# A quarter of the tokens leaves the dense expert loop and gathers its expert rows instead

## The reference, cut to what matters

```python
def peer_ffn(h, ...):
    ...
    top_s, pos = lax.top_k(cand_s, PEER_TOPK)
    eid = jnp.take_along_axis(cand_i, pos, axis=-1)      # 128 expert numbers per token
    gate = jax.nn.softmax(top_s, axis=-1)
    ...
    a = jnp.einsum('td,tkd->tk', hb, peer_u[eb], preferred_element_type=jnp.float32)
    a = jax.nn.gelu(a, approximate=False)
    return jnp.einsum('tk,tkd->td', (gb * a).astype(hb.dtype), peer_v[eb])
```

## Time and profile before

| | us |
|---|---|
| median of 3 runs | 1116.73 (1114.97 to 1119.02) |
| the profiled execution | 1120.11, of which the span of the trace is 1118.3 |
| start up to the choice of experts | 0 to 200 |
| choice of experts | 200 to 289 |
| gates | 289 to 392 |
| expert loop | 392 to 1112 |
| tail | 1112 to 1118 |

### The profile page before, as it was taken

The page is one execution under the profiler, slowest core; times in us unless marked ns, Lnnn a source line. Parts: engine busy times, 40 slices in busy tenths (PEclk is TensorE's granted clock), DMA queues, the critical chain, the costliest instruction groups (busy, mean ns, idle before and its releaser), DMA issues.

```text
span 1118.3 us, 19162 instructions
## 1 busy us (share of the span) xinstructions
PE 1013.0 (91%) x6627; PEld 917.6 (82%) x6627; DVE 731.9 (65%) x1264; ACT 475.1 (42%) x762; POOL 217.6 (19%) x203
## 2 busy tenths in 40 slices
PE   6988998990466699999999999999999999999997
PEld 5878777880456699999999999999999999999996
DVE  4596415799899866666666666666666666666664
ACT  5543514111367754444444444444444444444442
POOL 2385003389399900000000000000000000000000
PEclk9989968996699999999999999999999999999999
DMA  6542102520000075555555555555555555555553
GB/s 189 177 134 98 46 31 76 166 99 0 1 0 0 1 242 186 188 182 187 184 185 185 185 187 185 185 186 187 185 185 187 186 188 186 189 186 186 188 188 132
DMA packets 63568, 163.75 MB, mean 146 GB/s; under 512 B 6036, under 2 KB 29608, under 8 KB 63544
## 3 DMA queue, kind: packets, MB, share of 16 engines
q1 hardware_dynamic: 63216, 163.37, 42.7%
q10 hardware_dynamic: 328, 0.08, 0.0%
HBM read 161.33 MB, written 2.10 MB: 146 GB/s over the span
## 4 chain that ended last, share of the span: by engine, by line
PE 65%; POOL 5%; issue 2%; DVE 1%; ACT 0%; POOLq 0%; DVEq 0%
PE psum L1066 33%; PE psum L1316 31%; POOL raw L1035 5%; PE psum L1291 1%; DVE rr L868 0%; DVE big L815 0%; DVE big L927 0%; DVE rr L820 0%; PE psum L1279 0%; ACT big L506 0%; POOLq L1043 0%; DVE big L826 0%; ACT rr L465 0%; ACT picks L495 0%; DVEq L89 0%
## 5 line engine op out<-in xcount | busy, mean ns | idle before, releaser
L1066 PEld LDWEIGHTS psum<-ht,rr 128*128 128x128 f32 x3168 | 397.0, 192 | 10.5 <-issue 0.7
L1066 PE MATMUL psum<-ht,rr 128*128 128x256 f32 x3168 | 400.7, 283 | 0.5 <-DVE rr L820 0.5
L1316 PE MATMUL psum<-rr 128*128 128x512 f32 x1536 | 372.3, 391 | 0.0
L1316 PEld LDWEIGHTS psum<-rr 128*128 128x128 f32 x1536 | 280.4, 188 | 52.9
L886 DVE TENSOR_TENSOR rr<-raw,rr 128x1024 fp32r<-128x1024 f32 x128 | 156.9, 1226 | 124.4 <-ACT rr L534 124.4
L534 ACT ACTIVATE rr<-raw 128x1024 fp32r<-128x1024 f32 x128 | 135.7, 1060 | 184.9 <-PE psum L1316 184.8
L820 DVE TENSOR_TENSOR rr<-raw,rr 128x1024 fp32r<-128x1024 f32 x128 | 156.0, 1219 | 10.1 <-ACT rr L465 10.1
L540 ACT ACTIVATE gel<-psum 128x256 f32<-128x256 f32 x128 | 49.0, 383 | 216.7 <-PE psum L1066 216.7
L465 ACT ACTIVATE rr<-raw 128x1024 fp32r<-128x1024 f32 x128 | 134.7, 1052 | 5.9 <-DMA raw<-in_peer_u_dram 5.9
L892 DVE TENSOR_TENSOR big<-big,gel 128x256 f32 (+1 forms) x128 | 54.5, 426 | 124.6 <-ACT gel L540 124.6
L1291 PE MATMUL psum<-raw,rr 128*128 128x128 f32 x512 | 67.3, 288 | 34.9 <-POOL raw L1035 16.2
(11 more groups left out here) (150 smaller groups left out, 608.5 us busy)
## 6 DMA issues: line engine op xcount, KB each, us to landing
raw<-in_peer_u_dram SPq DMA_DIRECT2D x128, 512.0 KB, 4.1
raw<-in_peer_v_dram SPq DMA_DIRECT2D x128, 512.0 KB, 3.6
big<-in_w_in_dram SPq DMA_DIRECT2D x10, 1024.0 KB, 7.2
big<-in_peer_wq_dram SPq DMA_DIRECT2D x8, 1024.0 KB, 5.6
big<-in_w_out_dram SPq DMA_DIRECT2D x4, 1024.0 KB, 5.6
big<-in_x_dram SPq DMA_DIRECT2D x2, 512.0 KB, 3.9
h_kept<-big SPq DMA_DIRECT2D x2, 512.0 KB, 7.6
raw<-h_kept SPq DMA_DIRECT2D x2, 512.0 KB, 3.7
```

The costliest lines, as they stand in the source:

```text
L1066: i = pe.matmul(dst, lhs(a, k), rhs(b, k), start=(n == 0), stop=(n == 3 * DK - 1))
L1316: i = pe.matmul(psum[:, 4 + 2 * t + n, :], g_sp[:, s, x, t * P:(t + 1) * P], v_sp[:, s, y, n * 512:(n + 1) * 512], start=(first and m == 0 ...
```

## The change

The tokens 192 to 255 (partitions 64 to 127 of the second token tile) leave the dense path. `gates`, `gel` and `g_sp` hold 192 tokens (`ND`), the gates stage has 24 groups, and `up` streams 192 columns. `down` does the first 128 tokens with six matmuls; the other 64 have their high and low parts side by side as 128 stationary columns, which takes four matmuls, and the two halves are added at the end by a matmul with a constant (`K_SUM`).

The 64 tokens have 64 x 128 choices, so 64 gathers (`N_GATHER`) of 128 rows, one row a partition: partition 64+t has the second half of token t's experts, partition t the first half. The tables lie as one, `peer_uv`, with u and v of an expert side by side (8 KB), so that a gather brings 1 MB. Three buffers (`GB`) go round. For gather g, in the blocks 2g and 2g+1:

- DVE `dot`: u part times the token's row (`hrow`), summed to one number a partition, at the end of its block 2g.
- ACT `dot_gelu`: Gelu of it, in block 2g+1 between `block_v` and `block_g`.
- POOL: times the gate (`p_coef`).
- ACT `scaled_v`: v part times that number, at the end of block 2g+1, behind `block_u`.
- POOL: adds it to `acc`, 128 x 1024, and then issues the gather g+3.

New in front of the loop: SP loads the norm's weights for all partitions (`g2row`), POOL makes `hrow` ahead of the first staircase, DVE and ACT put numbers and gates in place, SP moves the halves of three small tables to partitions 0 to 63, POOL issues three gathers ahead of its first `gated`. New behind it: ACT copies banks 6 and 7 out, PE adds `acc` and them up with four float32 matmuls. The loops of ACT and DVE are written out block by block instead of as a loop of two blocks; PE's and SP's are loops as before.

```diff
+NG = 64
+ND = SEQ - NG
+NQ, OHS = ND // GRP, 3
+N_GATHER, GB = PH * TOPK // 2, 3
...
+        at = NK * ND
+        acc = take(D)
+        guv = take(GB * 2 * D).rearrange("p (s d) -> p s d", s=GB)
+        hrow = take(D)
+        g2row = raw[:, 2 * D:3 * D]
+        g_id, g_gate, g_dot, g_coef = (sel[:, n, :] for n in range(4))
+        g_id = g_id.bitcast(mybir.dt.int32)
+        rows_uv = puv.rearrange("n m d -> (n m) d")
...
+        g_sp = rr[:, 8 * D:8 * D + 4 * ND].rearrange("p (s t a) -> p s t a", s=2, a=2)
...
             for t in range(2):
                 sp.dma_start(h_dram[t], xt[:, t, :]).then_inc(st_h, 16)
+            sp.wait_ge(pe_cat, 2)
+            sp.dma_start(g2row, g2[0:1, :].to_broadcast([P, D])).then_inc(ld_row, 16)
...
+            sp.wait_ge(p_row, 1)
+            sp.dma_start(hrow[0:NG, :], hrow[NG:P, :]).then_inc(ld_row, 16)
+            sp.wait_ge(d_sel, 1)
+            sp.dma_start(g_id[0:NG, :], eint[NG:P, 1].rearrange("p h k -> p (h k)")[:, 0:N_GATHER]).then_inc(ld_sel, 16)
+            sp.wait_ge(d_pick, PH + 1)
+            sp.dma_start(g_gate[0:NG, :], pick3[NG:P, 2, 1].rearrange("p h k -> p (h k)")[:, 0:N_GATHER]).then_inc(ld_sel, 16)
             for s in range(2):
                 sp.wait_ge(b_done, NQ - 1 + s)
-                sp.dma_start(v_raw[:, s, :], pv[s]).then_inc(ld_v[s], 16)
+                sp.dma_start(v_raw[:, s, :], puv[s, :, D:2 * D]).then_inc(ld_v[s], 16)
+            sp.dma_start(cst[:, :], const[:, K_SUM:N_CONST]).then_inc(ld_sum, 16)
...
+            def dot_gelu(g):
+                act.wait_ge(d_dot, g + 1)
+                act.activation(g_coef[:, g:g + 1], g_dot[:, g:g + 1], ACT.Gelu).then_inc(a_gc, 1)
+            def scaled_v(g):
+                act.wait_ge(p_coef, g + 1)
+                act.activation(guv[:, g % GB, D:2 * D] if g else acc, guv[:, g % GB, D:2 * D], ACT.Copy,
+                               scale=g_coef[:, g:g + 1]).then_inc(a_sv, 1)
 
             block_u(1, 1, 16, True)
-            for b in range(2):
-                block_v(b, b, True)
-                block_g(b, b, True)
-                block_u(b, b + 2, 32, False)
-            with act.Fori(1, NK // 2 - 1) as i:
-                for s in range(2):
-                    block_v(s, 2 * i + s, False)
-                    block_g(s, 2 * i + s, False)
-                    block_u(s, 2 * i + (s + 2), 16 * i + 32, False)
-            for b in range(NK - 2, NK):
-                block_v(b % 2, b, False)
-                block_g(b % 2, b, False)
+            for b in range(NK):
+                block_v(b % 2, b, b < 2)
+                if b % 2:
+                    dot_gelu(b // 2)
+                block_g(b % 2, b, b < 2)
+                if b + 2 < NK:
+                    block_u(b % 2, b + 2, 16 * (b // 2 + 2), False)
+                if b % 2:
+                    scaled_v(b // 2)
+            act.wait_ge(v_lo, NK)
+            act.wait_ge(c_done, NK)
+            for n in range(2):
+                act.activation(v_raw[:, 0, n * 512:(n + 1) * 512], psum[:, 6 + n, :], ACT.Copy).then_inc(a_yb, 1)
...
+            dve.wait_ge(d_seq, seq.up())
+            dve.scalar_tensor_tensor(eint[NG:P, 1], pick3[NG:P, 1, 1], float(NK), pick3[NG:P, 0, 1], ALU.mult, ALU.add)\
+               .then_inc(d_seq, 1)
+            dve.wait_ge(d_seq, seq.up())
+            dve.tensor_copy(g_id[NG:P, :], eint[NG:P, 1].rearrange("p h k -> p (h k)")[:, N_GATHER:]).then_inc(d_sel, 1)
...
+            def dot(g):
+                dve.wait_ge(ld_g[g % GB], 16 * (g // GB + 1))
+                dve.scalar_tensor_tensor(guv[:, g % GB, 0:D], guv[:, g % GB, 0:D], 1.0, hrow, ALU.mult, ALU.mult,
+                                         accum_out=g_dot[:, g:g + 1]).then_inc(d_dot, 1)
 
             block_u(1, 1)
             dve.wait_ge(b_ev, NQ)
-            expert_block(0, 0, first=True)
-            expert_block(1, 1, first=True)
-            with dve.Fori(1, NK // 2 - 1) as i:
-                for s in range(2):
-                    expert_block(s, 2 * i + s)
-            expert_block(0, NK - 2, last=True)
-            expert_block(1, NK - 1, last=True)
+            dve.wait_ge(ld_row, 32)
+            for b in range(NK):
+                block_v(b % 2, b)
+                block_g(b % 2, b, b < 2)
+                if b + 2 < NK:
+                    block_u(b % 2, b + 2)
+                if b % 2 == 0:
+                    dot(b // 2)
...
+            for n in range(2):
+                a = n * 512
+                dve.tensor_tensor(big[:, a:a + 512], raw[:, a:a + 512], psum[:, 4 + n, :], ALU.add).then_inc(d_out, 1)
+            for n in range(2):
+                a = D + n * 512
+                dve.wait_ge(pe_sum, n + 1)
+                dve.tensor_tensor(big[:, a:a + 512], raw[:, a:a + 512], psum[:, 1 + 2 * n, :], ALU.add).then_inc(d_out, 1)
...
+            pool.wait_ge(a_xs, 4)
+            pool.wait_ge(ld_row, 16)
+            pool.tensor_tensor(hrow, xs[:, 1, :], g2row, ALU.mult).then_inc(p_row, 1)
...
+            def gather(g):
+                pool.indirect_dma_start(guv[:, g % GB, :], None, rows_uv,
+                                        bass.IndirectOffsetOnAxis(ap=g_id[:, g:g + 1], axis=0)).then_inc(ld_g[g % GB], 16)
+            pool.wait_ge(d_pick, PH + 1)
+            pool.wait_ge(a_gate, 1)
+            pool.wait_ge(d_sel, 1)
+            pool.wait_ge(ld_sel, 32)
+            pool.wait_ge(pe_pk, 2)
+            for g in range(GB):
+                gather(g)
...
+            for g in range(N_GATHER):
+                pool.wait_ge(a_gc, g + 1)
+                pool.tensor_tensor(g_coef[:, g:g + 1], g_coef[:, g:g + 1], g_gate[:, g:g + 1], ALU.mult).then_inc(p_coef, 1)
+                pool.wait_ge(a_sv, g + 1)
+                if g:
+                    if g > 1:
+                        pool.wait_ge(p_acc, g - 1)
+                    pool.tensor_tensor(acc, acc, guv[:, g % GB, D:2 * D], ALU.add).then_inc(p_acc, 1)
+                if g + GB < N_GATHER:
+                    if g:
+                        pool.wait_ge(p_acc, g)
+                    gather(g + GB)
...
-                product(psum[:, 2 * s, 0:SEQ], lambda a, k: ut[:, s, a, k, :], lambda b, k: ht[:, b, k, :], a_done)
+                product(psum[:, 2 * s, 0:ND], lambda a, k: ut[:, s, a, k, :], lambda b, k: ht[:, b, k, 0:ND], a_done)
...
-                for t in range(2):
-                    for n in range(2):
-                        for m, (x, y) in enumerate(((0, 0), (0, 1), (1, 0))):
-                            i = pe.matmul(psum[:, 4 + 2 * t + n, :], g_sp[:, s, x, t * P:(t + 1) * P],
-                                          v_sp[:, s, y, n * 512:(n + 1) * 512], start=(first and m == 0), stop=(last and m == 2))
+                for n in range(2):
+                    for m, (x, y) in enumerate(((0, 0), (0, 1), (1, 0))):
+                        i = pe.matmul(psum[:, 4 + n, :], g_sp[:, s, 0:P, x], v_sp[:, s, y, n * 512:(n + 1) * 512],
+                                      start=(first and m == 0), stop=(last and m == 2))
+                for n in range(2):
+                    for y in range(2):
+                        i = pe.matmul(psum[:, 6 + n, :], g_sp[:, s, P:ND, :].rearrange("p t a -> p (t a)"), v_sp[:, s, y, n * 512:(n + 1) * 512],
+                                      start=(first and y == 0), stop=(last and y == 1))
                 i.then_inc(c_done, 1)
...
+            pe.wait_ge(ld_sum, 16)
+            pe.wait_ge(p_acc, N_GATHER - 1)
+            pe.wait_ge(a_gel, NK)
+            for n in range(2):
+                pe.matmul(psum[:, 1 + 2 * n, :], cst[:, P:2 * P], acc[:, n * 512:(n + 1) * 512], start=True, stop=False)
+            for n in range(2):
+                pe.wait_ge(a_yb, n + 1)
+                pe.matmul(psum[:, 1 + 2 * n, :], cst[:, 0:P], v_raw[:, 0, n * 512:(n + 1) * 512], start=False, stop=True)\
+                  .then_inc(pe_sum, 1)
```

More of the change, by code:

```diff
@@ L84, in up, with layer @@
         return self.n
-def layer(nc, x, meta, g1, w_in, gq, gk, pool_w, pool_s, w_out, g2, wq, sk1, sk2, pu, pv, const, out):
+def layer(nc, x, meta, g1, w_in, gq, gk, pool_w, pool_s, w_out, g2, wq, sk1, sk2, pu, puv, const, out):
     ctx = ExitStack()
@@ L97, in layer @@
         big = sb("big", [P, NK * SEQ])
-        gates = big[:, :].rearrange("p (n t) -> p n t", t=SEQ)
+        gates = big[:, 0:NK * ND].rearrange("p (n t) -> p n t", t=ND)
         rr = sb("rr", [P, 9 * D], F32R)
@@ L228, in layer @@
         d_g32, d_out = sem("d_g32"), sem("d_out")
+        ld_row, ld_sel, ld_sum = sem("ld_row"), sem("ld_sel"), sem("ld_sum")
+        ld_g = [sem(f"ld_uv{s}") for s in range(GB)]
+        d_sel, d_dot, a_gc, a_sv, a_yb = sem("d_sel"), sem("d_dot"), sem("a_gc"), sem("a_sv"), sem("a_yb")
+        p_row, a_gate, p_coef, p_acc, pe_sum = sem("p_row"), sem("a_gate"), sem("p_coef"), sem("p_acc"), sem("pe_sum")
         d_xs = sem("d_xs")
@@ L495, in _ @@
```

(3 more changed lines are left out.)

55 lines of the change are left out of this document (24 added, 31 removed).

## The result

| | before | after |
|---|---|---|
| median, us | 1117.88 (4 runs on this chip) | 1254.83 (1251.94 to 1257.55, 4 runs) |
| span of the profiled execution, us | 1118.3 | 1253.1 |
| up to the first up product of the loop, us | 391.9 | 372.1 |
| expert loop, us | 720.4 | 873.5 |
| tail, us | 6.0 | 7.5 |

The change makes the kernel slower: the ratio is 1.123, 95% interval 1.119 to 1.127. That is above the range of the prediction. The part ahead of the loop became 19.8 us shorter, the tail 1.5 us longer, the loop 153 us longer.

What follows compares the result with a forecast made beforehand. PE bounds the kernel before; after, a ring through the odd block's u load, 12.0 us a pair. From 1120.1: -15.6 outside the loop, +48.6 and -4 in it, 1149; median 3.4 lower, 1146 us; range 1045 to 1200.

Steps and rivals of the forecast that it cites:

- the ring: Expert loop: closed chain through the odd block's u load, scaled v and POOL's sum; 10.7 us a pair without the gather.
- the gather inside the ring: Expert loop: the gather's 1.05 MB make u land 1.3 us later, so a pair takes 12.0 us.
- the sum of 1149: Whole kernel, profiled execution: 1120.1 with -15.6, +48.6 and -4 gives 1149 us.
- The bound that I gave for just this: Upper bound of the gather step: whole gather ahead of u and starting late, 2.5 us more, 13.2 a pair.
- that rival: Slow gather in the loop: POOL takes longer or u waits; 12.5 to 13.6 us a pair, 1220 us; chance 0.15.
- 93 ns: PE in the loop: an up matmul with 192 columns takes 93 ns instead of 120, giving 9.05 us a pair.
- PE's rival at 962 us: Loop: PE stays the bound, POOL and DVE don't hinder each other; 9.05 us a pair, 962 us; chance 0.04.
- The exclusion: Loop, shared port: POOL and DVE exclude each other; of POOL's 2.2 us sum DVE loses 2.05.
- The port's 10.1 us a pair: Loop, port shared by DVE and POOL: 7.8 + 2.05 + 0.25 = 10.1 us; as a rival alone 1028 us, chance 0.08.
- The rest: Outside the loop: gates -24.4, their start +2.0, first staircase +4.2, short instructions +0.8, tail +1.8; together -15.6 us.
- The direction: Whole kernel: slower 0.55, faster 0.40, the same 0.05.
- a gather that costs the ring little: Loop rival: gather leaves u nearly alone; ring 10.7 to 11.4 us, 1085 us, range 1066 to 1110; chance 0.28.

Runs made afterwards that it cites:

- sp_u_first: Changed kernel with only SP's load order altered to u odd, v even, u even, v odd; 1029.2 us, ratio to before 0.921.
- small_sum: Changed kernel with POOL adding only 64 of the 1024 columns of the gathered v; 1145.2 us, ratio to before 1.024.
- act_sv_first: Changed kernel with the scaled v put ahead of the high part of u on ACT in the odd block; 1081.9 us, ratio to before 0.967.
- small_gather: Changed kernel with rows of 512 bytes (0.07 MB) from the fourth gather on, dot product times zero; 1103.2 us, ratio to before 0.987.
- half_gather: Changed kernel with rows of 4 KB (0.52 MB) from the fourth gather on, dot product times zero; 1179.8 us, ratio to before 1.054.
- dense_only: Changed kernel without the loop's gathers, dot products, coefficients, scaled v and sums; 1023.8 us, ratio to before 0.915.
- up128: Changed kernel without the gathered part, up streaming 128 columns instead of 192 from block 2 on; 1025.6 us, ratio to before 0.917.

## Why the prediction was wrong

**What bounds the kernel, and the ring.** Right, link for link. The chain after is the ring that was drawn, DVE's low part of v waits for POOL's sum in each pair, and nearly always only the odd block's load is in the chain. sp_u_first opened the ring and took 3.65 us from a pair; POOL's sum is a link (small_sum), and the place behind `block_u` makes it one (act_sv_first).

**The step that failed** is the gather inside the ring: "all is moved at 7.2: u lands 1.3 us later and the ring is 12.0 us". Counted from the end of POOL's sum (705.51 us), predicted against measured: low part of v done 1.23, 1.09; u issued 1.94, 1.88; u landed 7.54, 8.93; scaled v done 9.7, 11.05; next sum done 12.0, 13.51. The 1.4 us are all in the landing, and 64 pairs of 13.61 instead of 12.0 make 103 us of the 106 by which the profiled execution exceeds the sum of 1149.

The term that was mis-sized is what the gather adds to the landing of u. Its 1.05 MB need 2.5 us at the rate of the earlier trace rows, and the step charged u 1.3 of them: the gather was to begin at 2.2 us, at full rate, before v and u had anything to move, and so to have 1.2 us of its transfer hidden. Nothing was hidden. The gather's instruction holds POOL for 1.66 us from 705.78; v moves ahead of it; its own first packets come after 709.5, 4.0 us behind the end of the sum; and u has it in front of itself whole. Between 707.7 and 709 all queues together moved 0.19 MB, where the step had 0.55: by an estimate from these rows, 0.85 us of the 1.4. Another 0.35 us may be the 0.15 MB that the next block's load of v had moved before u was down.

When the gather starts is not the whole of it. In small_sum it leaves POOL at 713.57, ahead of v, its first packets follow after 714.0, and u still takes 7.11 us. So the simple reading of small_gather and half_gather is the one to keep: all of the gather's bytes, at full rate. The prediction's remark that u "shares with a transfer that was issued first" is not borne out, since the two went one behind the other, but it is not the error in the number either: the sum had u come down behind all 2.1 MB already.

The bound that I gave for just this ("all of it in front of u and starting late", 13.2 us, 1220 us) was the value to take, and 13.6 was the upper end of its range. It had 0.15. Of the other half of that rival, numbers and descriptors that take POOL longer, the runs show a part: the instruction takes 0.98 us in small_sum, where it begins ahead of DVE's subtraction, and 1.66 in the changed kernel, where it begins with 0.8 us of it to go. The prediction had less than 0.3 us for such a wait. Whether these 0.7 us cost anything in the ring no run shows.

**PE.** 93 ns was wrong, 110 to 111 is measured; the row of 16 stationary columns reached down to 120 ns only, as the text said, and I went past it. In the changed kernel this cost nothing, since PE was off the path. In dense_only, up128 and sp_u_first, where the ring is open or gone, it is the bound: 9.96 us a pair, not 9.05; PE's rival at 962 us could not have come. Nor was the clock at full throughout, as the prediction had it: over the loop it was 0.93.

**DVE and its port.** The exclusion held: 2.55 us for 1.23 beside a sum of 2.38. The port's 10.1 us a pair was an overestimate: in sp_u_first the pair takes 9.96 us with the sum in it, and PE is busy throughout. There the two wait for each other in turn: POOL's sum, begun at 708.76 in the midst of a DVE subtraction, takes 2.97 us, and DVE's next subtraction, begun at 709.66, takes 3.15 and ends 1.1 us behind the sum. PE is not held up by either. The product with the gate, 0.28 predicted, took 0.87 us and ended with the DVE instruction beside it; it is hidden too.

**The rest** came to -18.3 us where -15.6 was predicted, and that they are so near is partly luck. The rows that answer to the earlier trace rows, then to the earlier trace rows, then to the earlier trace rows:

```profile
192.62 1.05 SPq L311 DMA_DIRECT2D h_kept<-big  x2
203.13 2.39 POOL L1038 TENSOR_TENSOR big<-big,raw 128x1024 f32<-128x1024 f32 x1 [9.67 <-DMA raw<-in_norm_g_dram]
205.48 1.23 POOL L1043 TENSOR_TENSOR big<-big 128x32 f32<-128x32 f32 x7
206.75 0.33 DVE L815 MAX8 big<-big 128x8 f32<-128x50 f32 x2 [7.28 <-POOL big L1043]
```
```profile
299.54 3.03 POOL L1082 TENSOR_TENSOR raw<-rr,picks 128x512 f32<-128x512 f32 x3
```
```profile
1249.40 0.69 DVE L971 TENSOR_TENSOR big<-raw,psum 128x512 f32<-128x512 f32 x1 [0.17 <-PE psum L1422]
```

The first staircase started 0.45 us late instead of 4, but not because the wait was short. The load of the norm's weights landed 10.5 us behind the issue of the stores of h, where the prediction had 8.4, and DVE stood idle for 7.28 us instead of 1.35: 5.9 us, where 4.2 was predicted and 6 was the bound. This execution had issued those stores 5.5 us earlier than the kernel before (192.62 for 198.11), with a granted clock of 1.00 from 186 to 194 us where the other had 0.58. In the ten other runs, which share this part, they were issued at 195.6 to 199.2 us, and the staircase started at 208.5 to 212.0. Without that head start the rest would have come to about -12.8 (an estimate). The three gathers ahead of the gates held POOL until 299.5 us (292.96 before, and 1.5 us of that from the later start): about 5 us, outside the bounds of 0 to 4, but partly made good by the buffers: the stage took 80.1 us, 24 groups of 3.05 and 6.9 instead of the 3.8 of before, so 3.1 us where the prediction had 2.0. The tail took 1.5 us more for 1.8.

**The direction** (slower, 0.55) came out right. The weight of 0.28 on a gather that costs the ring little rested on the mean use of the DMA alone, and half_gather shows that half of the gather's bytes already cost 1.2 us a pair.

## What to carry to other kernels

A new transfer is not free because the DMA is half idle: ask which load is issued within some microseconds of it and who waits for that load, and if the answer is a ring, add the whole transfer, at full rate, to that ring. Where loads stand in one queue with waits, issue them in the order in which their buffers come free; here that order alone, of four loads in SP's loop, was worth 18% of the changed kernel. A matmul with 128 stationary columns did not get shorter below 110 ns, so fewer moving columns pay only as long as the matmul takes longer than that: from 256 to 192 columns a matmul gained 9 ns and not 27.
